# One free slot between two steps of the compressed attention, and cross-attention scores formed up to four units ahead

## The chip, the core and the metric

The kernel runs on one core of a Trainium2 chip. The core has TensorE (PE: matrix products, which are also used to turn tiles over), VectorE (DVE), ScalarE (ACT), GpSimd (POOL) and a queue (SP) that issues the loads. Each engine works through its own instructions in the order of the program and waits at semaphores for the others. The metric is device time in microseconds (us), median of the runs; lower is better.

## What is computed

Two layers of a first block, then two layers of a second block, on 512 rows of width 1024, all in float32:

```python
for i in range(DEPTH):                       # first block, DEPTH = 2
    ...                                      # projections, gated linear recurrence
    s_cmp = jnp.einsum('bgntd,bgcd->bgntc', q_nope, kc) * scale      # 31 compressed keys
    p_cmp = masked_softmax(s_cmp, cmp_mask)
    o_cmp = jnp.einsum('bgntc,bgcd->bgntd', p_cmp.astype(vc.dtype), vc)
    o_slc = selected_attn(q_rope, k_sl, heads(vsl, KVH), sel, scale)
    o_win = window_attn(q_rope, k_wn, heads(vwn, KVH), scale)
    o_nsa = gates[0] * o_cmp + gates[1] * o_slc + gates[2] * o_win
    ...
for l in range(DEPTH):                       # second block
    ...                                      # mixer
    s = jnp.einsum('bshd,bmhd->bhsm', q, k).astype(jnp.float32) * (XA_HEAD_DIM ** -0.5)
    p = jax.nn.softmax(s, axis=-1).astype(v.dtype)                   # 4 heads, 256 memory rows
    o = jnp.einsum('bhsm,bmhd->bshd', p, v).reshape(B, S, D_MODEL)   # and o @ wo
    ...                                      # feed-forward
```

## The kernel before

A product of float32 numbers is made of three products of parts: high times high, high times low, low times high. So every operand is split in two. A weight chunk of 128x1024 is loaded by SP into `raw`, its high part is cut by ACT (L2010) and its low part by POOL (L2682). A tile that TensorE has turned over (matrix product with `ident`, L762 and L1037 in block one, L1758 in block two) is read from its PSUM bank by ACT, which writes the high part, and then by DVE, which writes the low part (L1392, L2265). Only after DVE's read is the bank free ("evacuated").

The work of each layer is a list of steps, made by `steps_one` and `steps_two`. All five engines walk through the same list, and each does its part of every step (`step_...` functions of the same name for each engine). A step placed later in the list is thus later on every engine. A PSUM bank is given to each tile in advance: tiles with the same set of banks take turns, and a tile may be written only when the one before it in that bank has been evacuated (class `Groups`).

**Block one, attention.** `attention_steps` writes the list in slots. One slot holds in most cases: `turn` (a 128x128 piece of the shares of four heads is turned over), `exp` of the scores of the slot before, `recip`, one or two `score` (row j, PE L1023, L1024, L1026), `weigh` (DVE L1717 makes a factor, POOL L2674 multiplies the row by it), at most one step of the list `compressed`, and `value` (three products with the turned shares, L1050 to L1052) of the turn two slots earlier. The first turn of a unit waits for POOL's multiplication of the unit's last row (`pn_ready`). There are 40 turns, numbered `t`, for 4 tiles of 128 queries (`qt`).

For every `qt` there are four compressed steps, one in each of four slots in a row: `c_score` (PE L993, then DVE), `c_exp` (ACT L1318), `c_weigh` (six DVE instructions, L1688 to L1693) and `c_turn` (PE L1003: eight turns of the weighted shares into two banks, then ACT L1123 copies them). TensorE's `c_turn` waits for `cp_ready`, which the last of the six DVE instructions (L1693, 128x248 into `decays`) gives. The tiles of `c_turn`, of `c_score` and of `turn` take turns in the banks 7, 0, 1.

**Block two, cross-attention.** A unit is one head `hh` and one tile `qt` of 128 queries: 16 units, `u = 4 * hh + qt`. Four things are done for a unit: `scores(u)` (PE L1959, six products of 128x256), `greatest(u)` (DVE L2528) and `probs(u)` (ACT L2211, exponential into `Px`), `shares(u)` (DVE L2534 and L2535, division by the sum), `probs_turn(u)` (PE L1758, two turns, banks 3 and 4 in turn) with ACT L2062 and DVE L2265 (`PxT`) reading them out. Step `("xatt", hh, qt)` forms the scores of unit u + 2 and turns the shares of unit u + 1; DVE does shares(u + 1), greatest(u + 2) and the reading of unit u. Step 3 and below are mixed with chunks of other products (L1869, L1803), steps 6 and 7 are followed by one chunk of the queries of the last head each (`xq`, 24 products, L1803), and after each head comes `xout` (L1991, 12 products of 128x512, which need all four `PxT` of the head). Steps 8 to 15 have nothing between them but `xout`.

Of the kernel before, what the change touches and what calls it, by code (L numbers as in the profile page):

```python
# [210 lines left out]
def attention_steps():  # L211
# [10 lines left out]

    weighed, sent = set(), set()
    while t < len(TURNS):
        if not out:
            compressed = [("c_score", 0), ("c_exp", 0), ("c_weigh", 0), ("c_turn", 0)]
# [4 lines left out]
        if turned:  # L231
            slot += [("turn", t)]
            t += 1
            if qt and kt == 0 and (g, br) == (0, 0):
                compressed = [(kind, qt) for kind in ("c_score", "c_exp", "c_weigh", "c_turn")]
# [14 lines left out]
        slot += compressed[:1]  # L250
# [177 lines left out]

def groups_two(step):
# [28 lines left out]
    if kind == "xatt":  # L458
        hh, qt = step[1:]
        return [(("xs", hh, qt), (0, 1)), (("xp", hh, qt), (3, 4))]  # L460
# [5 lines left out]
def build(nc, d, out, counts):  # L466
# [3 lines left out]
    with ExitStack() as ctx:  # L470
# [169 lines left out]
        Px = sb("Px", [P, 2, MEM], where=xat)  # L640
# [1107 lines left out]
        def tensor_two(pe, l):  # L1748
# [214 lines left out]
            def probs_turn(u):  # L1963
                name = ("xp", *divmod(u, TT))
                pe.wait_ge(*px_ready.at(l, u + 1))
                turn(name, MT, lambda i: Px[:, u % 2, i * P:(i + 1) * P])

            def step_xatt(step):
                hh, qt = step[1:]
                u = hh * TT + qt  # L1970
                if u == 0:
                    pe.wait_ge(*G.evacuated(("xk", KD - 1), l))
                    scores(0)
                    scores(1)
                    probs_turn(0)
                if u + 2 < XH * TT:
                    scores(u + 2)
# [34 lines left out]
        def scalar_two(act, l):  # L2012
# [195 lines left out]
            def probs(u):  # L2208
                name = ("xs", *divmod(u, TT))
                act.wait_ge(*nm_ready[1].next(l))  # L2210
                nc.scalar.activation(Px[:, u % 2, :], G.ps(name)[:, 0:MEM], ACT.Exp, bias=nmx[:, u % 4:u % 4 + 1],  # L2211
# [7 lines left out]
            def step_xatt(step):  # L2219
                hh, qt = step[1:]  # L2220
                u = hh * TT + qt
                if u == 0:
                    probs(0)
                    probs(1)
                turned(u)
                if u + 2 < XH * TT:
                    probs(u + 2)
# [16 lines left out]
        def vector_two(dve, l):  # L2244
# [285 lines left out]
            def shares(u):  # L2530
# [4 lines left out]
                ts(Px[:, u % 2, :], Px[:, u % 2, :], recx[:, c], None, ALU.mult).then_inc(*px_ready.up())  # L2535

            def step_xatt(step):
                hh, qt = step[1:]
                u = hh * TT + qt
                if u == 0:  # L2540
                    greatest(0)
                    greatest(1)
                    shares(0)
                if u + 1 < XH * TT:
                    shares(u + 1)
                if u + 2 < XH * TT:
                    greatest(u + 2)
# [293 lines left out]
```

## Time and profile before

| | us |
|---|---|
| median of 3 runs (3026.43 to 3032.96) | 3026.7 |
| the profiled execution | 3025.9 |
| its span in the trace | 3024.0 |
| TensorE busy in the span | 2798.5 |
| VectorE busy | 1227.6 |
| ScalarE busy | 1284.9 |
| GpSimd busy | 1153.1 |

The profile is that of one execution. Its span is the time from the first to the last recorded instruction; 1.9 us of the run's time lie outside it. Times in the trace are counted from the start of the span. "Idle before" an instruction is the time in which its engine had nothing to do, and the name behind the arrow is what ended it. The mean granted clock of TensorE over the span was 0.964 of its full speed, which has two levels: 2.4 GHz (1.0) and 1.2 GHz (0.5).

### The profile page before, as it was taken

How to read it: one execution, taken by the hardware profiler on the slowest of the kernel's cores; microseconds unless marked ns; L12 is line 12 of the kernel's file. 1: busy time of each engine (PE TensorE's matmuls, PEld its weight loads, DVE VectorE, ACT ScalarE, POOL GpSimd, SP SyncE). 2: the span in 40 equal slices, each digit the busy share in tenths (PEclk: the TensorE clock that was granted, in tenths of full speed). 3: DMA queues.
4: the chain of work that ended last, by engine and by line, in shares of the span. 5: the costliest groups of instructions: out<-in, count | busy, mean ns of one | idle time of the engine just before them, and what ended most of it. 6: DMA issues, size and time to landing. Idle time of an engine off the chain costs nothing.

```text
span 3024.0 us, 40461 instructions
## 1 busy us (share of the span) xinstructions
PE 2798.5 (93%) x13636; PEld 2326.6 (77%) x13636; DVE 1227.6 (41%) x2186; ACT 1284.9 (42%) x2191; POOL 1153.1 (38%) x537
## 2 busy tenths in 40 slices
PE   8978789998778999899998999999899999899998
PEld 6777658777765788688786888888678887788887
DVE  4755771375567223434333331322442423232132
ACT  4443653554465353353443442334244444243243
POOL 3313334331234343244452344444234444244442
PEclk9989799999979999999999999999999999999999
DMA  5212102321210232133331233333223333133333
GB/s 148 63 44 63 42 1 84 96 70 37 64 56 1 63 109 83 42 98 105 105 112 49 84 105 98 98 98 109 63 75 93 91 116 101 56 93 103 91 98 98
DMA packets 269778, 242.32 MB, mean 80 GB/s; under 512 B 29376, under 2 KB 201600, under 8 KB 269568
## 3 DMA queue, kind: packets, MB, share of 16 engines
q1 hardware_dynamic: 266672, 235.12, 26.9%
q10 hardware_dynamic: 2896, 4.52, 0.5%
q8 instruction: 118, 1.93, 0.3%
q14 instruction: 92, 0.75, 0.1%
HBM read 237.51 MB, written 2.10 MB: 79 GB/s over the span
## 4 chain that ended last, share of the span: by engine, by line
issue 47%; PE 25%; POOL 25%; DVE 1%; ACT 1%; POOLq 0%; DMA 0%; DVEq 0%; ACTq 0%
POOL wlo L2682 23%; PE bank L1869 4%; PE bank L1873 4%; PE bank L1872 4%; PE bank L1807 3%; PE bank L1803 3%; PE bank L1806 3%; PE bank L1758 1%; POOL Ql L2674 0%; PE bank L1991 0%; POOL dE L2674 0%; POOL Kl L2674 0%; PE bank L1037 0%; POOLq L2681 0%; POOL vv L2674 0%
## 5 line engine op out<-in xcount | busy, mean ns | idle before, releaser
L2682 POOL TENSOR_TENSOR wlo<-raw,whi 128x1024 fp32r<-128x1024 f32 (+2 forms) x440 | 1057.4, 2408 | 1684.4 <-ACT whi L2010 1684.2
L2010 ACT CAST whi<-raw 128x1024 fp32r<-128x1024 f32 (+2 forms) x443 | 456.1, 1034 | 710.9 <-PE bank L1869 465.8
L1803 PE MATMUL bank<-xhi,whi 128*128 128x512 f32 x928 | 365.3, 394 | 0.3 <-issue 0.3
L1807 PE MATMUL bank<-xhi,wlo 128*128 128x512 f32 x928 | 363.1, 391 | 0.0
L1806 PE MATMUL bank<-xlo,whi 128*128 128x512 f32 x928 | 363.0, 391 | 0.0
L1869 PE MATMUL bank<-whi,xhi 128*128 128x512 f32 x832 | 329.2, 396 | 9.7 <-POOL wlo L2682 5.8
L1872 PE MATMUL bank<-wlo,xhi 128*128 128x512 f32 x832 | 326.4, 392 | 0.0
L1873 PE MATMUL bank<-whi,xlo 128*128 128x512 f32 x832 | 326.2, 392 | 0.0
L776 PE MATMUL bank<-whi,xhi 128*128 128x512 f32 (+2 forms) x704 | 263.3, 374 | 3.1 <-DVE pT L1392 3.1
L779 PE MATMUL bank<-wlo,xhi 128*128 128x512 f32 (+2 forms) x704 | 257.7, 366 | 0.0
L780 PE MATMUL bank<-whi,xlo 128*128 128x512 f32 (+2 forms) x704 | 257.2, 365 | 0.0
L1803 PEld LDWEIGHTS bank<-xhi,whi 128*128 128x128 f32 x928 | 175.4, 189 | 38.0 <-issue 1.7
L1807 PEld LDWEIGHTS bank<-xhi,wlo 128*128 128x128 f32 x928 | 175.2, 189 | 36.8
L1806 PEld LDWEIGHTS bank<-xlo,whi 128*128 128x128 f32 x928 | 175.4, 189 | 36.1
L1869 PEld LDWEIGHTS bank<-whi,xhi 128*128 128x128 f32 x832 | 157.7, 190 | 44.1 <-POOL wlo L2682 6.6
L1873 PEld LDWEIGHTS bank<-whi,xlo 128*128 128x128 f32 x832 | 157.6, 189 | 33.3
L1872 PEld LDWEIGHTS bank<-wlo,xhi 128*128 128x128 f32 x832 | 157.9, 190 | 32.1
L776 PEld LDWEIGHTS bank<-whi,xhi 128*128 128x128 f32 x704 | 136.2, 194 | 24.8 <-DVE pT L1392 3.6
L780 PEld LDWEIGHTS bank<-whi,xlo 128*128 128x128 f32 x704 | 135.1, 192 | 20.9
L779 PEld LDWEIGHTS bank<-wlo,xhi 128*128 128x128 f32 x704 | 135.7, 193 | 19.4
L2374 DVE TENSOR_TENSOR h<-h,bank 128x512 f32<-128x512 f32 x64 | 44.0, 688 | 249.6 <-PE bank L1873 249.6
L1869 PE MATMUL bank<-whi,gT 128*128 128x512 f32 x352 | 137.4, 390 | 1.6 <-DVE et L2367 1.6
(492 smaller groups left out, 4995.9 us busy)
## 6 DMA issues: line engine op xcount, KB each, us to landing
raw<-in_w_in SPq DMA_DIRECT2D x147, 512.0 KB, 3.7
raw<-in_w SPq DMA_DIRECT2D x132, 512.0 KB, 3.8
raw<-in_w_pg SPq DMA_DIRECT2D x16, 512.0 KB, 3.8
raw<-in_w_o SPq DMA_DIRECT2D x16, 512.0 KB, 3.8
raw<-in_xa_k SPq DMA_DIRECT2D x16, 512.0 KB, 3.9
raw<-in_xa_v SPq DMA_DIRECT2D x16, 512.0 KB, 3.8
raw<-in_xa_q SPq DMA_DIRECT2D x16, 512.0 KB, 4.0
raw<-in_xa_o SPq DMA_DIRECT2D x16, 512.0 KB, 3.8
```

The source lines that it names most:

```text
L776: mm = pe.matmul(o, a, wh, start=(i == 0 and kk_ == 0), stop=False)
L779: pe.matmul(o, a, wl, start=False, stop=False)
L780: mm = pe.matmul(o, b, wh, start=False, stop=(i == n - 1 and kk_ == nk - 1))
L1803: mm = pe.matmul(o, wh, rhs[0][:, k, :], start=(k == 0), stop=False)
L1806: pe.matmul(o, wh, rhs[1][:, k, :], start=False, stop=False)
L1807: mm = pe.matmul(o, wl, rhs[0][:, k, :], start=False, stop=(k == KD - 1))
L1869: mm = pe.matmul(G.ps(name)[:, :], a, wh, start=(i == 0 and kk_ == 0), stop=False)
L1872: pe.matmul(G.ps(name)[:, :], a, wl, start=False, stop=False)
L1873: mm = pe.matmul(G.ps(name)[:, :], b, wh, start=False, stop=(i == n - 1 and kk_ == nk - 1))
L2010: nc.scalar.copy(whi[:, j % SLOTS, 0:nk * cols], raw[:, j % SLOTS, 0:nk * cols]).then_inc(hi_split, 1)
L2374: tt_(at, at, G.ps(name)[:, :], ALU.add).then_inc(*G.empty(name))
L2682: nc.gpsimd.tensor_tensor(wlo[:, s, 0:n], raw[:, s, 0:n], whi[:, s, 0:n].bitcast(F32), ALU.subtract).then_inc(lo_split, 1)
```

## The change

In block one an empty slot (`None`) is put between `c_weigh` and `c_turn`. In block two the scores run ahead by up to four units instead of two, but only from step 4 on: `scored_to` gives the last unit whose scores are formed by step u. Steps 0 to 3 form the same units as before, step 4 forms 6 and 7, step 5 forms 8 and 9, steps 6 to 11 one each, steps 12 to 15 none. The score tiles of units 6 and above take turns in the banks 2, 7, 0, 1 instead of 0, 1, and `Px` has four places instead of two.

```diff
+    def compressed_steps(qt):
+
+        return [("c_score", qt), ("c_exp", qt), ("c_weigh", qt), None, ("c_turn", qt)]
...
-        slot += compressed[:1]
+        slot += compressed[:1] if compressed and compressed[0] else []
         compressed = compressed[1:]
...
+def scored_to(u):
+
+
+    return min(u + (2 if u < 4 else 3 if u == 4 else 4), XH * TT - 1)
+
+
+def scored_in(u):
+    return range(scored_to(u - 1) + 1 if u else 0, scored_to(u) + 1)
...
-        return [(("xs", hh, qt), (0, 1)), (("xp", hh, qt), (3, 4))]
+        return [(("xs", *divmod(u, TT)), (0, 1) if u < 6 else (2, 7, 0, 1)) for u in scored_in(hh * TT + qt)] + [(("xp", hh, qt), (3, 4))]
...
-        Px = sb("Px", [P, 2, MEM], where=xat)
+        Px = sb("Px", [P, 4, MEM], where=xat)
...
-                    scores(0)
-                    scores(1)
-                    probs_turn(0)
-                if u + 2 < XH * TT:
-                    scores(u + 2)
+                for v in scored_in(u):
+                    scores(v)
+                    if v == 1:
+                        probs_turn(0)
                 if u + 1 < XH * TT:
                     probs_turn(u + 1)
...
-                if u == 0:
-                    greatest(0)
-                    greatest(1)
-                    shares(0)
-                if u + 1 < XH * TT:
-                    shares(u + 1)
-                if u + 2 < XH * TT:
-                    greatest(u + 2)
+                for v in scored_in(u):
+                    if v > 1:
+                        shares(v - 1)
+                    greatest(v)
+                    if v == 1:
+                        shares(0)
+                if scored_to(u) == XH * TT - 1 and len(scored_in(u)):
+                    shares(XH * TT - 1)
                 at = (slice(None), slice(None), slice(qt * P, (qt + 1) * P))
```

ScalarE's `step_xatt` reads out the turned tile of unit u first and then takes the exponentials of the units of `scored_in(u)`.

Below, lines of the changed kernel have numbers 13 or 14 higher than the same lines before.

TensorE, block one, slot of turn 27 (`qt` 3), before, from the score's last product (`causal`): the turns of `c_turn` (source `decays`) stand right behind it, ahead of the value products (source `Pt`).

```order
L1026 MATMUL bank<-causal,identb 128x128
L1001 REGISTER_ALU [waits cp_ready]
L1003 MATMUL bank<-ident,decays 31x128 [waits emptied1]
L1003 MATMUL bank<-ident,decays 31x128 x3
L1001 REGISTER_ALU
L1003 MATMUL bank<-ident,decays 31x128 [waits emptied7]
L1003 MATMUL bank<-ident,decays 31x128 x3
L1050 MATMUL bank<-Pt,vhi 128x512 [waits emptied1]
L1051 MATMUL bank<-Pt,vlo 128x512
L1052 MATMUL bank<-Pt,vhi 128x512
L1034 REGISTER_ALU
L1035 REGISTER_ALU [waits pn_ready]
```

The same place now, from the first value product on:

```order
L1064 MATMUL bank<-Pt,vhi 128x512 [waits emptied1]
L1065 MATMUL bank<-Pt,vlo 128x512
L1066 MATMUL bank<-Pt,vhi 128x512
L1048 REGISTER_ALU
L1051 MATMUL bank<-ident,Ql 128x128 [waits emptied1,pn_ready]
L1051 MATMUL bank<-ident,Ql 128x128
L1051 MATMUL bank<-ident,Kl 128x128 x2
L1034 REGISTER_ALU
L1037 MATMUL bank<-khh,qhl 128x512 [waits emptied4]
L1038 MATMUL bank<-kll,qhl 128x512
L1040 MATMUL bank<-causal,identb 128x128
L1015 REGISTER_ALU [waits cp_ready]
```

Three value products, one turn (which waits for POOL, `pn_ready`) and one score have moved ahead of `c_turn` and its wait. The DVE work of `c_weigh` has not moved.

TensorE, block two, from the end of `xout` of head 0 through steps 4 and 5, before (`kx8,qx8` are scores, `ident,Px` the turns of the shares):

```order
L1991 MATMUL bank6<-PxT,vx 128x512 x6
L1954 REGISTER_ALU
L1959 MATMUL bank0<-kx8,qx8 128x256 x6
L1965 REGISTER_ALU
L1758 MATMUL bank4<-ident,Px 128x128 x2
L1954 REGISTER_ALU
L1959 MATMUL bank1<-kx8,qx8 128x256 x6
L1965 REGISTER_ALU
L1756 REGISTER_ALU
L1758 MATMUL bank3<-ident,Px 128x128 x2
```

and now:

```order
L2004 MATMUL bank6<-PxT,vx 128x512 x6
L1968 REGISTER_ALU
L1973 MATMUL bank2<-kx8,qx8 128x256 x6
L1968 REGISTER_ALU
L1973 MATMUL bank7<-kx8,qx8 128x256 x6
L1979 REGISTER_ALU
L1772 MATMUL bank4<-ident,Px 128x128 x2
L1968 REGISTER_ALU
L1970 REGISTER_ALU
L1973 MATMUL bank0<-kx8,qx8 128x256 x6
L1968 REGISTER_ALU
L1973 MATMUL bank1<-kx8,qx8 128x256 x6
```

The scores of units 6 and 7 stand ahead of the first turn, those of 8 and 9 ahead of the next one (bank 3, behind the last row shown); before, it was one unit's scores ahead of each turn.

VectorE, block two, from the first division of step 4, before (`nmx` is the greatest score, `recx` the reciprocal of the sum, `PxT` the reading of the turned tile):

```order
L2535 TENSOR_SCALAR Px<-Px,recx 128x256
L2528 TENSOR_REDUCE nmx<-bank0 128x1
L2262 REGISTER_ALU
L2265 TENSOR_TENSOR PxT<-bank3,PxT 128x2x128
L2532 REGISTER_ALU
L2534 RECIPROCAL recx<-sumx 128x1
L2252 REGISTER_ALU
L2535 TENSOR_SCALAR Px<-Px,recx 128x256
L2528 TENSOR_REDUCE nmx<-bank1 128x1
```

and now:

```order
L2548 TENSOR_SCALAR Px<-Px,recx 128x256
L2540 REGISTER_ALU
L2541 TENSOR_REDUCE nmx<-bank2 128x1
L2545 REGISTER_ALU
L2547 RECIPROCAL recx<-sumx 128x1
L2265 REGISTER_ALU
L2548 TENSOR_SCALAR Px<-Px,recx 128x256
L2540 REGISTER_ALU
L2541 TENSOR_REDUCE nmx<-bank7 128x1
L2275 REGISTER_ALU
L2278 TENSOR_TENSOR PxT<-bank3,PxT 128x2x128
```

The reading of a turned tile (`PxT`), which frees bank 3 or 4, now stands behind a second division and a second search for the greatest. It is so in steps 4 and 5; in step 11 it stands behind one more division.

## Rows read from the trace of the kernel before

**Rows 1.** The page: the span and TensorE's busy time.

```profile
span 3024.0 us, 40461 instructions
PE 2798.5 (93%) x13636; PEld 2326.6 (77%) x13636; DVE 1227.6 (41%) x2186; ACT 1284.9 (42%) x2191; POOL 1153.1 (38%) x537
```

**Rows 2.** Waits of PE, whole span: us in total, times, longest us.

```profile
PE bank L1758 <- DVE Px L2535: 25.8, 24, 2.3
PE bank L1003 <- DVE decays L1693: 19.4, 8, 3.1
```

**Rows 3.** Timeline, layer 0, `qt` 1, PE: start us, us, instruction [idle before].

```profile
371.51 1.53 PE L1003 MATMUL bank<-ident,decays 128*31 128x128 f32 x8 [3.08 <-DVE decays L1693]
...
376.32 0.60 PE L1037 MATMUL bank<-ident,vv 128*128 128x128 f32 x4
```

**Rows 4.** Timeline, the same place, DVE and POOL.

```profile
369.15 0.41 DVE L1688 SCALAR_TENSOR_TENSOR decays<-k_cbias,decays 128x248 f32<-128x248 f32 x1
...
371.29 0.68 DVE L1392 TENSOR_TENSOR Pt<-bank,Pt 128x512 fp32r<-128x512 f32 x1
...
369.31 1.14 POOL L2674 TENSOR_TENSOR vv<-vv,coef 128x512 f32<-128x512 f32 x1 [2.72 <-DVE coef L1717]
```

**Rows 5.** Timeline, layer 0, `qt` 3, PE and POOL.

```profile
425.94 1.14 POOL L2674 TENSOR_TENSOR Kl<-Kl,coef 128x512 f32<-128x512 f32 x1 [2.71 <-DVE coef L1717]
...
428.13 1.06 PE L1003 MATMUL bank<-ident,decays 128*31 128x128 f32 x8 [2.97 <-DVE decays L1693]
...
429.72 0.38 PE L1037 MATMUL bank<-ident,Ql 128*128 128x128 f32 x2
...
431.45 0.38 PE L1037 MATMUL bank<-ident,Ql 128*128 128x128 f32 x2
```

**Rows 6.** Timeline, layer 0, `qt` 2, PE.

```profile
396.91 1.06 PE L1003 MATMUL bank<-ident,decays 128*31 128x128 f32 x8 [2.76 <-DVE decays L1693]
...
402.94 0.43 PE L1037 MATMUL bank<-ident,dE 128*128 128x128 f32 x2 [0.56 <-POOL Ql L2674]
```

**Rows 7.** Timeline, layer 0, `qt` 0, PE.

```profile
348.23 1.91 PE L1003 MATMUL bank<-ident,decays 128*31 128x128 f32 x8 [0.87 <-DVE decays L1693]
...
354.32 0.65 PE L1037 MATMUL bank<-ident,Ql 128*128 128x128 f32 x4 [1.42 <-POOL Ql L2674]
```

**Rows 8.** Timeline, layer 0, cross-attention from step 4 on, PE.

```profile
1606.64 0.87 PE L1959 MATMUL bank<-kx,qx 128*128 128x256 f32 x6
1608.67 0.44 PE L1758 MATMUL bank<-ident,Px 128*128 128x128 f32 x2 [1.15 <-DVE Px L2535]
...
1620.46 0.43 PE L1758 MATMUL bank<-ident,Px 128*128 128x128 f32 x2 [1.99 <-DVE Px L2535]
...
1627.84 2.88 PE L1991 MATMUL bank<-PxT,vx 128*128 128x512 f32 x12
...
1637.88 3.02 PE L1991 MATMUL bank<-PxT,vx 128*128 128x512 f32 x12 [0.23 <-DVE PxT L2265]
...
1647.55 5.04 PE L1991 MATMUL bank<-PxT,vx 128*128 128x512 f32 x12 [1.00 <-DVE PxT L2265]
```

**Rows 9.** Timeline, the same stretch, DVE.

```profile
1608.86 0.41 DVE L2265 TENSOR_TENSOR PxT<-bank,PxT 128x256 fp32r<-128x256 f32 x1
1609.58 0.17 DVE L2534 RECIPROCAL recx<-sumx 128x1 f32<-128x1 f32 x1 [0.30 <-ACT Px L2211]
...
1611.09 0.17 DVE L2534 RECIPROCAL recx<-sumx 128x1 f32<-128x1 f32 x1 [0.30 <-ACT Px L2211]
```

**Rows 10.** Timeline, layer 1, cross-attention, PE.

```profile
2561.16 0.87 PE L1959 MATMUL bank<-kx,qx 128*128 128x256 f32 x6
...
2574.95 0.43 PE L1758 MATMUL bank<-ident,Px 128*128 128x128 f32 x2 [1.99 <-DVE Px L2535]
...
2580.73 2.88 PE L1991 MATMUL bank<-PxT,vx 128*128 128x512 f32 x12
...
2601.03 4.51 PE L1991 MATMUL bank<-PxT,vx 128*128 128x512 f32 x12 [1.00 <-DVE PxT L2265]
```

More of the change, by code:

```diff
@@ L225, in attention_steps @@
         if not out:
-            compressed = [("c_score", 0), ("c_exp", 0), ("c_weigh", 0), ("c_turn", 0)]
+            compressed = compressed_steps(0)
         slot = []
@@ L234, in attention_steps @@
             if qt and kt == 0 and (g, br) == (0, 0):
-                compressed = [(kind, qt) for kind in ("c_score", "c_exp", "c_weigh", "c_turn")]
+                compressed = compressed_steps(qt)
         slot += [("exp", i) for i in scored]
@@ L1965, in probs_turn @@
                 pe.wait_ge(*px_ready.at(l, u + 1))
-                turn(name, MT, lambda i: Px[:, u % 2, i * P:(i + 1) * P])
+                turn(name, MT, lambda i: Px[:, u % 4, i * P:(i + 1) * P])
             def step_xatt(step):
@@ L2210, in probs @@
                 act.wait_ge(*nm_ready[1].next(l))
-                nc.scalar.activation(Px[:, u % 2, :], G.ps(name)[:, 0:MEM], ACT.Exp, bias=nmx[:, u % 4:u % 4 + 1],
+                nc.scalar.activation(Px[:, u % 4, :], G.ps(name)[:, 0:MEM], ACT.Exp, bias=nmx[:, u % 4:u % 4 + 1],
                                      accum_out=sumx[:, u % 4:u % 4 + 1]).then_inc(*G.empty(name))
@@ L2221, in step_xatt @@
                 u = hh * TT + qt
-                if u == 0:
-                    probs(0)
-                    probs(1)
-                turned(u)
-                if u + 2 < XH * TT:
-                    probs(u + 2)
+                for v in scored_in(u):
+                    if v == u + 2 or (v > 1 and v == scored_in(u)[0]):
+                        turned(u)
+                    probs(v)
+                if not len(scored_in(u)):
+                    turned(u)
             def step_xout(step):
@@ L2534, in shares @@
                 link(nc.vector.reciprocal(recx[:, c], sumx[:, c]))
-                ts(Px[:, u % 2, :], Px[:, u % 2, :], recx[:, c], None, ALU.mult).then_inc(*px_ready.up())
+                ts(Px[:, u % 4, :], Px[:, u % 4, :], recx[:, c], None, ALU.mult).then_inc(*px_ready.up())
             def step_xatt(step):
@@ L2539, in step_xatt @@
                 u = hh * TT + qt
-                if u == 0:
-                    greatest(0)
-                    greatest(1)
-                    shares(0)
-                if u + 1 < XH * TT:
-                    shares(u + 1)
-                if u + 2 < XH * TT:
-                    greatest(u + 2)
+                for v in scored_in(u):
+                    if v > 1:
[5 more added lines that the diff above has]
+                    shares(XH * TT - 1)
                 at = (slice(None), slice(None), slice(qt * P, (qt + 1) * P))
```

## The prediction

> **What bounds the kernel now.** TensorE does: it is busy for 93% of the span, the next engine for 42% [rows 1]. So I read the list of its waits first: only what shortens a wait of TensorE, or lets it run at its higher clock, can move the time. The two largest entries that the change touches are the turns of the cross-attention shares (L1758 waiting for the division L2535, 25.8 us in 24 waits) and the turns of the compressed shares (L1003 waiting for L1693, 19.4 us in 8 waits) [rows 2]. The change removes no work, so 45.2 us is about all that is at stake, apart from the clock. Then the timeline around each wait, for every engine that feeds it: the question there is what is late next.
>
> **Block one: the eight waits of `c_turn`.** I take `qt` 1, 2, 3 and 0 in turn; layer 1 repeats layer 0 (8 waits, 19.4 us, against 9.7 us in the four rows of layer 0 [rows 3, 5, 6, 7]).
>
> `qt` 1. TensorE stands idle for 3.08 us up to 371.51 [rows 3], that is from 368.43, while DVE works through the six instructions of `c_weigh`, which began at 369.15 and made room for the next one at 371.29 [rows 4]. The edit leaves those where they are and puts a value product, a turn and a score ahead of TensorE's wait. Their price, from `qt` 3: turn, score and value together take 431.45 - 429.72 = 1.73 us, `c_turn` with its value product 429.72 - 428.13 = 1.59 us [rows 5]; half of the latter is the value (0.8), so turn and score are 0.9. The value product can run at once, to 369.2. The turn is the first of a unit and waits for POOL's row, which ends at 369.31 + 1.14 = 370.45 [rows 4]: a new, shorter wait of 1.2 us. Turn and score end at 371.4, when `cp_ready` is there, `c_turn` and a value end at 373.0, and the next turn, which needs its bank read by DVE (L1392, now directly behind `c_weigh` and once more behind ScalarE's copy), starts at about 373.3. Before, it started at 376.32 [rows 3]: 3.0 us saved. About half of that is clock: 371.51 to 376.32 is 4.8 us, while the same instructions took 3.3 us at `qt` 3 [rows 3, 5].
>
> `qt` 3. Idle from 425.16. Value to 425.96, POOL's row ready at 425.94 + 1.14 = 427.08, turn and score to 428.0, `c_turn` and value to 429.7, next turn 429.9 against 431.45 [rows 5]: 1.55 us saved. `qt` 2: value, turn and score (1.7 us) fit into the idle 2.76 us without a new wait for POOL, because this turn is not the first of a unit, and the factor that POOL waits for before 402.94 comes earlier too [rows 6]: 1.7 us. `qt` 0: there is 0.87 us in front of `c_turn` and 1.42 us in front of a turn that hangs on the same delayed scores [rows 7]; ScalarE's two copies now stand behind four exponentials, so I take 1.5 of the 2.3.
>
> Sum for a layer: 1.5 + 3.0 + 1.7 + 1.55 = 7.75 us, for two 15.5 us. Bounds: 19.4 + 2 x 1.5 (clock) = 22.4 if no new wait arose; 8 us if DVE and ScalarE, which have their own queues of turned tiles, hold back half of the shift. The other cost is nil: the copies are needed by `c_val`, which for `qt` 1 now comes one slot after `c_turn` instead of two, with some 1.3 us left.
>
> **Block two: steps 4 to 15.** Steps 0 to 3 are as before, so the waits in them stay. I count from the scores of step 4 (1606.64 in layer 0, 2561.16 in layer 1 [rows 8, 10]). One round of division, search for the greatest and exponential takes 1611.09 - 1609.58 = 1.5 us, and the reading of the turned tile (`PxT`) at 1608.86 to 1609.27 stands ahead of the second round [rows 9]. Now it stands behind it, and turns alternate between two banks, so the turn of step u + 1 waits for `PxT` of step u - 1:
> - Step 4: turn at +2.0 as before (same division, 1608.67 [rows 8]). Step 5: two scores of 0.7 to 0.9 us, to +3.7; the bank comes free at 2.6 + 1.5 = +4.2.
> - Step 6: `PxT` of step 5 is two rounds later, +7.3, while TensorE is ready at +5.2: a new wait of 2.1 us. The chunk behind it starts at +7.5.
> - Step 7: chunk 5.6, score 0.9, and no wait for the division, where 1.99 us stood before 1620.46. The next chunk starts at +14.1, as before, with two units' scores already made.
> - `xout` of head 1 at +19.8; before 1627.84 - 1606.64 = +21.2 in layer 0 and 2580.73 - 2561.16 = +19.6 in layer 1. The two layers differ by clock alone: the same 1.99 us of idle time was followed by 7.4 us up to `xout` in layer 0 and by 5.8 us in layer 1 [rows 8, 10].
> - Steps 8 to 11: each turn waits for a `PxT` round (0.6 to 1.0 us), and `PxT` of step 11 comes behind one more division, so `xout` of head 2 waits for it 2.5 us: 2.7 + 8.5 = 11.2 us from one `xout` to the next, before 1637.88 - 1627.84 = 10.0.
> - Steps 12 to 15 have only turns left: 6.4 us to the last `xout`, before 1647.55 - 1637.88 = 9.7.
>
> Together 19.8 + 11.2 + 6.4 = 37.4 us up to the last `xout`, before 40.9 and 39.9 [rows 8, 10]. The last `xout` itself was busy for 5.04 and 4.51 us where the others took 2.88 [rows 8, 10]: lower clock. With one stretch at the lower clock in each layer (1.6 us, from 7.4 against 5.8 above) it is 37.4 + 2.9 + 1.6 = 41.9, before 45.9 and 44.4: 4.0 and 2.5 us saved, 6.5 in all. Bounds: 45.9 + 44.4 - 2 x 40.3 = 9.7 us if no stretch falls; -3 us if each layer has two more of them and one more round than I count.
>
> On the clock the Trainium skill (TensorE: Matmul & The Clock Gate, Part 1: The HAM clock gate) says that the monitor looks at windows that run free of the kernel and do not begin anew with it. That fits the two layers above, with equal idle time and 1.6 us between them. By that rule no term of clock is safe, neither the 2 x 1.5 us of `qt` 1 nor the 1.6 us of each layer.
>
> **Sum.** 15.5 + 6.5 = 22.0 us. The profiled execution took 3025.9 us, so 3003.9; the median of the runs is 0.8 above it: 3004.7 us. `Px` has more room and the loads of weights are not moved: POOL had nothing to do before its chunk, and the chunks follow TensorE.
>
> **Rivals.**
> - Cross-attention gives nothing (chance 0.2): the new waits behind `PxT` are as long as the ones removed. The 2.1 and 2.5 us above speak for it, the bare last four steps (9.7 to 6.4) against. Time: 3026.7 - 15.5 = 3011.2.
> - The clock takes some back (0.15): the half-speed stretch of `qt` 1 stays in both layers (3.0), and one more falls in each cross-attention (3.2). Time: 3004.7 + 6.2 = 3010.9. For it: the new waits of 2.1 and 2.5 us are longer than the 1.99 us that went before the stretch in layer 0. Against: two of the waits of `c_turn`, of 2.76 and 2.97 us, were followed by `c_turn` at 1.06 us for eight, the full speed. This is what the rule of the page cited above would do here.
> - Block one moves its wait to DVE and ScalarE (0.12): half the gain, 8 us, with 6.5: 3012.2.
> - Both small (0.05): the wait stands one slot on, and cross-attention gives nothing; 3022.
> - Slower (0.04): one mechanism, the place of `PxT` behind a second division. If each of the seven turns of steps 5 to 11 stood one whole round (1.5 us) later than it did before and the last four gave nothing, it would cost 2 x 7 x 1.5 = 21 us, more than the 15.5: 3032. It decides from 1.1 us for a turn. Against it: the second round comes only in steps 4, 5 and 11; from step 6 on each step has one round, as before, and so has time to catch up.
>
> **How the numbers follow.** The forecast has 0.44. The range is to hold 8 in 10: down to 3026.7 - 22.4 - 5 = 2999, up to 3018, past the three first rivals; outside are both small, slower, and a part of the tails. A measurement of this kernel can tell about 0.2%, 6 us, from no change. Faster than 3020.7 are the forecast and the first three rivals less a tail: 0.88; within 0.2% 0.08; slower 0.04.
>
> **What would show it.** In the trace after: waits of L1017 (the new line of `c_turn`) of 1 us in all or less, new waits of about 1.2 us of the first turn of a unit for POOL at `qt` 1 and 3, and the attention of each layer 7 to 8 us shorter. In cross-attention: no wait for the division in steps 4 to 15 but that of step 4 (1.1 us), new waits of L1772 and of `xout` for `PxT` of about 2 us, and the last two `xout` 6 to 7 us apart. Wrong if the value product ahead of `c_turn` waits, if DVE reads its tiles no earlier after `qt` 1, or if `xout` of head 2 waits for more than 4 us.

## The result, and the profile after

| | before | after | ratio (95% interval) |
|---|---|---|---|
| median of 6 runs each, us | 3026.1 | 3005.6 | 0.9935 (0.992 to 0.9951) |
| runs, us | 3017.7 to 3033.0 | 3003.7 to 3008.9 | |
| span of the profiled execution, us | 3024.0 | 3001.9 | |

The forecast was 3004.7 us. The total came out within 1 us, but its terms did not all do so: in the traced execution block two gave 3.1 us of the 6.5 it was meant to give, and time in code that no edit touches made up for it.

The page of the kernel after, with the span and the busy time of the engines, beside [rows 1]:

```profile
span 3001.9 us, 40477 instructions
PE 2793.4 (93%) x13636; PEld 2321.5 (77%) x13636; DVE 1225.8 (41%) x2186; ACT 1283.4 (43%) x2191; POOL 1154.6 (38%) x537
```

The list of TensorE's waits after the change (us in total, times, longest us), beside [rows 2]. Lines have moved by 13 or 14: L1758 is L1772 now, L1003 is L1017, L1991 is L2004, L2265 is L2278, L2535 is L2548, L1693 is L1707:

```profile
PE bank L1772 <- DVE PxT L2278: 10.5, 12, 1.9
PE bank L1772 <- DVE Px L2548: 9.5, 6, 2.3
...
PE bank L2004 <- DVE PxT L2278: 6.7, 4, 2.3
...
PE bank L1017 <- DVE decays L1707: 2.3, 2, 1.1
```

The 19.4 us in front of `c_turn` are down to 2.3. The 25.8 us of waiting for the division are down to 9.5, but 17.2 us of waiting for `PxT` stand there now, where 2.6 us stood before: of 16.3 us taken from one wait, 14.6 came back in another.

**Where the 22.1 us of the two spans lie.** I compared the start of the same matmul, counted from the start of the program, in both traces; both have 13636 matmuls. A stretch's gain is how much closer its two ends stand. The second column is the changed kernel profiled once more.

| stretch (us in the trace before) | first trace after | second trace after | predicted |
|---|---|---|---|
| attention, layer 0 (339 to 450) | 7.5 | 7.3 | 7.75 |
| attention, layer 1 (882 to 996) | 7.3 | 8.0 | 7.75 |
| cross-attention from step 4, layer 0 (1606.6 to 1653.5) | 1.8 | 1.7 | 4.0 |
| cross-attention from step 4, layer 1 (2561.2 to 2607) | 1.3 | 1.3 | 2.5 |
| all the rest | 4.2 | -1.4 | 0 |
| the two spans | 22.1 | 16.9 | 22.0 |

The rest holds no instruction that the change moves. It is made mostly of pieces of 0.6 to 3.1 us of either sign, most of them where a stretch at the lower clock stands in one trace and not in the other, and it changed sign between two traces of one kernel.

**Block one after.** Timeline of layer 0, PE, at `qt` 1 (the first three rows), `qt` 2 and `qt` 3, and then POOL at `qt` 1 (columns as in [rows 3]):

```profile
368.41 0.66 PE L1051 MATMUL bank<-ident,vv 128*128 128x128 f32 x4 [1.33 <-POOL vv L2687]
...
369.40 1.15 PE L1017 MATMUL bank<-ident,decays 128*31 128x128 f32 x8
...
371.12 0.66 PE L1051 MATMUL bank<-ident,vv 128*128 128x128 f32 x4
...
391.75 1.15 PE L1017 MATMUL bank<-ident,decays 128*31 128x128 f32 x8 [1.15 <-DVE decays L1707]
...
420.08 0.44 PE L1051 MATMUL bank<-ident,Ql 128*128 128x128 f32 x2 [1.23 <-POOL Kl L2687]
...
421.11 1.11 PE L1017 MATMUL bank<-ident,decays 128*31 128x128 f32 x8
```

```profile
367.21 1.14 POOL L2687 TENSOR_TENSOR vv<-vv,coef 128x512 f32<-128x512 f32 x1 [2.72 <-DVE coef L1731]
```

`c_turn` waits for nothing at `qt` 1 and `qt` 3. The turn ahead of it waits 1.33 and 1.23 us for POOL: new waits, less than half as long as the 3.08 and 2.97 us in [rows 3, 5]. `c_turn` took 1.53 us in [rows 3] and takes 1.15 us here. The stretch at the lower clock behind the long wait, 371.9 to 375.3 us in the trace before, is gone: both traces without the slot (before, and block two alone below) have it in both layers, and none of the ten with one slot has it.

**Cross-attention after, from step 4's scores on.** PE, layer 0, then layer 1, beside [rows 8, 10]:

```profile
1587.07 1.59 PE L1973 MATMUL bank<-kx,qx 128*128 128x256 f32 x12
1589.09 0.44 PE L1772 MATMUL bank<-ident,Px 128*128 128x128 f32 x2 [0.43 <-DVE Px L2548]
...
1591.27 0.44 PE L1772 MATMUL bank<-ident,Px 128*128 128x128 f32 x2 [0.31 <-DVE PxT L2278]
...
1594.30 0.44 PE L1772 MATMUL bank<-ident,Px 128*128 128x128 f32 x2 [1.88 <-DVE PxT L2278]
...
1606.44 2.88 PE L2004 MATMUL bank<-PxT,vx 128*128 128x512 f32 x12
...
1617.65 5.49 PE L2004 MATMUL bank<-PxT,vx 128*128 128x512 f32 x12 [2.34 <-DVE PxT L2278]
...
1624.87 0.77 PE L1772 MATMUL bank<-ident,Px 128*128 128x128 f32 x4 [1.40 <-DVE PxT L2278]
1626.64 4.60 PE L2004 MATMUL bank<-PxT,vx 128*128 128x512 f32 x12 [1.00 <-DVE PxT L2278]
```

```profile
2540.42 1.59 PE L1973 MATMUL bank<-kx,qx 128*128 128x256 f32 x12
...
2561.41 2.88 PE L2004 MATMUL bank<-PxT,vx 128*128 128x512 f32 x12
...
2572.63 4.38 PE L2004 MATMUL bank<-PxT,vx 128*128 128x512 f32 x12 [2.34 <-DVE PxT L2278]
...
2580.50 3.01 PE L2004 MATMUL bank<-PxT,vx 128*128 128x512 f32 x12 [0.99 <-DVE PxT L2278]
```

The first two waits are short, then come 1.88 and 2.34 us for `PxT`. Right behind the second one the `xout` of head 2 takes 5.49 and 4.38 us; before the change it took 3.02 and 3.03. That is the lower of the two clocks: the view by stretches (stretch, us, busy time and count of PE, PEld, DVE, ACT and POOL, granted clock, DMA share, GB/s) gives a mean granted clock of 0.65 of full speed from 1617 to 1631, so the lower level held for some 70% of it.

```profile
1617.00:1631.00 14.00, 10.96 (x30) 8.20 (x31) 4.02 (x9) 3.02 (x7) 0.00 (x0) 0.65 0.00 1
```

### The profile page after: what moved, and what is told of

Read it like the earlier page. It is cut to its first block, busy times and chain, and to the rows that moved or that the text cites. A ratio compares the mean times of both kernels' runs of the same rounds, so it can differ in the third digit from the quotient of the medians.

```text
span 3001.9 us, 40477 instructions
## 1 busy us (share of the span) xinstructions
PE 2793.4 (93%) x13636; PEld 2321.5 (77%) x13636; DVE 1225.8 (41%) x2186; ACT 1283.4 (43%) x2191; POOL 1154.6 (38%) x537
## 4 chain that ended last, share of the span: by engine, by line
issue 47%; POOL 25%; PE 25%; DVE 1%; ACT 1%; POOLq 0%; DMA 0%; DVEq 0%; ACTq 0%
POOL wlo L2695 23%; PE bank L1883 4%; PE bank L1886 4%; PE bank L1887 4%; PE bank L1821 3%; PE bank L1820 3%; PE bank L1817 3%; PE bank L1772 1%; POOL Ql L2687 0%; PE bank L2004 0%; POOL vv L2687 0%; POOL dE L2687 0%; POOL Kl L2687 0%; POOL At L2687 0%; POOLq L2694 0%
```

## The experiments

### The two parts alone, and both again

Block one alone is the kernel before with

```
+    def compressed_steps(qt):
+
+        return [("c_score", qt), ("c_exp", qt), ("c_weigh", qt), None, ("c_turn", qt)]
...
-        slot += compressed[:1]
+        slot += compressed[:1] if compressed and compressed[0] else []
```

and block two alone is the changed kernel without the `None`.

> The kernel before with the empty slot alone; block two as before. Theory (parts add up, and what is left over is clock): each layer's attention is 7.2 to 7.5 us shorter, as in the trace after the change (14.7 us for two), so 3026 - 15 = 3011 us, ratio 0.995; what the difference to 3005.6 leaves, some 5 us, is block two with 3 and a clock that stands differently in stretches that no edit touches. The attention gives 14 to 15.5 us whatever the total does. Rival (the slot gives all of it, and cross-attention nothing): 3006 us, ratio 0.9935, and the 4 us of shift that the trace shows between the two attentions' end and cross-attention come back here. Rival (the clock gain of qt 1 is chance): one of the two layers gives 1.5 us less.

> The changed kernel without the empty slot: scores four units ahead alone. Theory: cross-attention from step 4 on gives 1 to 3 us a layer and no more, since waits for PxT take the place of waits for the division: 3026 - 3 = 3023 us, ratio 0.999; the last three xout stand 11.2 us and, at the higher clock, 6.4 us apart, with some 1.5 us more for each xout at the lower clock. As predicted: 6.5 us, 3019.5 us, ratio 0.9978. Rival (nothing): 3026 us and 1.0.

> The changed kernel again, on the chip and beside the runs of before that the parts alone have. Theory: ratio 0.9935 as before, the sum of the two parts alone within 3 us; the attention of block one gives 14.7 us again, cross-attention from step 4 on 1 to 4 us, and the shift outside both, 4.3 us in the first trace, comes out differently, between -4 and +5 us. Rival (the shift outside is a consequence of the change): it is 4 us again, with the stretches at the lower clock in the same places.

All beside the same runs of before (3025.9 us, 17 runs). The last two columns are how many us shorter a stage is than in the trace before:

| | median, us | ratio (95%) | attention, two layers | cross-attention from step 4, layers 0 and 1 |
|---|---|---|---|---|
| block one alone | 3012.5 (6 runs) | 0.9958 (0.9944 to 0.9973) | 14.7 in all | -0.2, -1.8 |
| block two alone | 3019.8 (12 runs) | 0.9981 (0.9971 to 0.999) | 0.0 and -3.5 | 2.6, 1.3 |
| both again | 3007.2 (6 runs) | 0.9935 (0.9921 to 0.9949) | 15.3 in all | 1.7, 1.3 |

13.4 and 6.1 us make 19.5, and both together give 18.7: the parts add up. Block one is worth 14.7 to 15.3 us in all three traces that have it, against the trace before. That the slot gives the whole falls: with it alone the ratio is 0.9958, and its interval leaves out 0.9935. But the trace before is one trace. The trace of block two alone runs the same attention without the slot, and its layer 1 took 3.5 us more: behind the waits of 2.75 and 2.97 us at `qt` 2 and 3 `c_turn` took 1.91 us, at the lower clock, where the trace before has 1.05 us behind waits of the same length. Against that trace the slot gives 18 us.

```profile
939.98 1.91 PE L1017 MATMUL bank<-ident,decays 128*31 128x128 f32 x8 [2.75 <-DVE decays L1707]
...
973.17 1.91 PE L1017 MATMUL bank<-ident,decays 128*31 128x128 f32 x8 [2.97 <-DVE decays L1707]
```

For block two the median (6.1 us) is near the forecast of 6.5, while the traces show 2.6 and 1.3 us in the two stages. The row of block one alone shows one reason why a trace is a poor yardstick here: its cross-attention runs the same instructions as the kernel before, and from step 4 on they took 0.2 and 1.8 us longer than in the profiled execution of before, with 10.2 us of granted half clock in each layer where that one had 10.2 and 6.8. Against this second trace the changed order gains 1.9 and 3.1 us, 5 in all. With the trace of the kernel with two empty slots below, four traces have the new order (from the scores of step 4 to the first matmul behind the last `xout`, 44.2 to 45.2 us in layer 0 and 44.5 to 44.7 in layer 1) and two the old (46.9 and 47.1, 45.8 and 47.6): the means differ by 4.4 us for the two layers. So block two gives 3 to 6 us, and one trace can't say more.

### Is it the place of `PxT` on DVE?

In the changed kernel DVE reads a step's turned tile behind all rounds of division and search for the greatest in that step; steps 4, 5 and 11 have two of the former. The next kernel puts the reading (`low()`) behind the first:

```
...
                 for v in scored_in(u):
                     if v > 1:
                         shares(v - 1)
                     greatest(v)
...
+                    if u > 3 and v == scored_in(u)[0]:
+                        low()
...
+                if u < 4 or not len(scored_in(u)):
+                    low()
```

> The changed kernel, with DVE's reading of the turned tile (PxT) in steps 4, 5 and 11 ahead of the second round of division and search for the greatest, no longer behind it. Theory (the turn of step u + 1 and xout wait for PxT behind the second round): the 1.88 us wait of the turn of step 6 falls to 0.3 to 0.7, the 2.34 us wait of xout of head 2 to about 1.2, together 2.5 to 3 us a layer, so 5 to 6 us less than the changed kernel, ratio to the kernel before 0.9918. Rival (the round itself is the bound: PE waits for DVE's rounds of 1.5 us wherever PxT stands): the waits move to the next turns and the total stays, 0 to 1 us a layer. Rival (the clock takes it): the waits go, and the xout of heads 2 and 3 stay at 4.4 to 5.5 us.

2999.0 us (5 runs), ratio 0.9908 (0.9893 to 0.9924), beside 3007.2 of both again on the same chip: 8.2 us less. PE's rows, layer 0 and then layer 1:

```profile
1600.06 0.44 PE L1772 MATMUL bank<-ident,Px 128*128 128x128 f32 x2 [0.90 <-DVE PxT L2278]
...
1612.26 2.88 PE L2004 MATMUL bank<-PxT,vx 128*128 128x512 f32 x12
...
1622.29 3.01 PE L2004 MATMUL bank<-PxT,vx 128*128 128x512 f32 x12 [1.15 <-DVE PxT L2278]
...
1628.80 4.60 PE L2004 MATMUL bank<-PxT,vx 128*128 128x512 f32 x12 [1.00 <-DVE PxT L2278]
...
2570.09 3.01 PE L2004 MATMUL bank<-PxT,vx 128*128 128x512 f32 x12 [1.15 <-DVE PxT L2278]
...
2576.60 3.03 PE L2004 MATMUL bank<-PxT,vx 128*128 128x512 f32 x12 [1.00 <-DVE PxT L2278]
```

The waits fell as expected, 1.88 to 0.90 and 2.34 to 1.15, and they did not move elsewhere: the place of `PxT` was the cause of that part of them. But the stages became 6.9 and 7.0 us shorter than before the change, 5.2 and 5.7 more than both again, where 2.5 to 3 were expected. The waits make 2.5 us a layer of it (0.31 + 0.98 + 1.19). The other 5.9 us of the 10.9 go with the clock: the `xout` of head 2 is back at 3.01 us, and the half clock from step 4 on fell from 17.0 us in both layers together to 3.4. These 13.6 us at half speed cost at most 6.8 us of time (an estimate: all of them spent on matmuls). With the full clock, the last two `xout` stand 6.5 us apart in both layers; the forecast had 6.4.

Then the two places apart: this kernel moves the reading in step 11 alone, and leaves the 1.88 us of step 6.

```
+                    if u == 11:
+                        low()
...
+                if u != 11:
+                    low()
```

> The changed kernel, with the reading of PxT ahead of the last division in step 11 alone; steps 4 and 5 stay as the change made them. It asks whether the wait of 2.34 us right in front of the xout of head 2 decides that xout's clock (4.35 to 5.49 us in six of six stages with that wait, 3.01 to 3.03 us in six of six with a wait of 0.23 to 1.15 us). Theory (it does): wait 1.15 us, the xout takes 3.0 us in both layers, head 3's follows 6.5 us later; with 1.2 us for the wait and 1.5 to 2.6 us for the clock that is 2.7 to 3.8 us a layer from step 4 on, 5.5 to 7.5 us in all against the changed kernel. Rival (the gaps of steps 4 to 7, of 1.88 us, bring the clock down later): the xout of head 2 stays at 4.4 us or more in at least one layer, and only 1.2 us a layer is gained.

3000.5 us (4 runs), ratio 0.9917 (0.99 to 0.9933), beside 3026.3 us of before (7 runs), as for the next three kernels. The `xout` of head 2 took 3.02 and 3.01 us behind a wait of 1.15 us. The gap of step 6 stands, so it is not that gap that lowers the clock there. Shortening the wait in front of that `xout` alone brought its clock back in both layers. The stages are 5.4 and 2.2 us shorter than before, 3.6 and 0.9 more than both again: in layer 1 the 1.2 us of the wait and the 1.4 us of this `xout` are partly eaten by a last `xout` of 4.60 us, where both again had 3.01.

### Earlier still

```
+                if u > 4:
+                    low()
                 for v in scored_in(u):
```

> The changed kernel, with the reading of PxT ahead of all rounds of its step from step 5 on (in step 4 behind the first). Theory (a turn waits for nothing but the PxT of the turn before last): the waits of 0.9 us in step 6 and of 0.88, 0.37 and 0.37 us behind the xout of head 1 go, but the xout of head 2 then stands behind the rounds of DVE, 1.5 us each, and comes 8.9 instead of 10.0 us after that of head 1; together 2 us a layer less than with the tile behind the first round: 3005.6 - 8 - 4 = 2994 us, ratio 0.989. Rival (the rounds bound these steps already): no more than tile behind the first round, 2999 us, ratio 0.991.

2998.8 us (4 runs), ratio 0.9917 (0.99 to 0.9933): no gain over the reading behind the first round (0.9908), as the rival said. My theory missed: the turns behind the `xout` of head 1 now wait 0.96 and 0.96 us, and the next `xout` comes 11.0 us after it, not 8.9. DVE, ScalarE and PE in this kernel:

```profile
1610.75 0.15 DVE L2547 RECIPROCAL recx<-sumx 128x1 f32<-128x1 f32 x1
...
1611.20 0.42 DVE L2541 TENSOR_REDUCE nmx<-bank 128x1 f32<-128x256 f32 x1
1612.51 0.42 DVE L2278 TENSOR_TENSOR PxT<-bank,PxT 128x256 fp32r<-128x256 f32 x1 [0.89 <-ACT PxT L2075]
1612.86 0.15 DVE L2547 RECIPROCAL recx<-sumx 128x1 f32<-128x1 f32 x1
```

```profile
1611.65 0.47 ACT L2224 ACTIVATE Px<-bank,nmx 128x256 f32<-128x256 f32 x1 [1.60 <-DVE nmx L2541]
...
1612.12 0.36 ACT L2075 CAST PxT<-bank 128x256 fp32r<-128x256 f32 x1
```

```profile
1617.29 4.49 PE L2004 MATMUL bank<-PxT,vx 128*128 128x512 f32 x12 [1.75 <-DVE PxT L2278]
```

The reading of `PxT` waits for ScalarE's copy of the same tile, and on ScalarE that copy is queued behind the next exponential, which waits for DVE's search. With the tile first, a round is search, exponential, copy, reading, division in a row: 1612.86 - 1610.75 = 2.11 us, where it was 1.5 us with the reading beside the exponential. The `xout` waited 1.75 us and took 4.49 and 4.37 us.

### One turn ahead of `xout`

The kernel with `PxT` behind the first round, and in the plan the first step of head 3 ahead of the `xout` of head 2:

```
+            if (hh, qt) != (3, 0):
+                s += [("xatt", hh, qt)] + (xv1[qt:qt + 1] if hh == 0 else [])
...
-        s += [("xout", hh)]
+        s += [("xatt", 3, 0)] * (hh == 2) + [("xout", hh)]
```

> The changed kernel with PxT read behind the first round, and the step of head 3's first tile ahead of the xout of head 2 on all engines. Theory (the 1.5 us wait of a turn behind that xout is DVE's, which reads the two banks of xout before it comes to PxT): that wait goes, the one of 1.0 us before the last xout stays, since a turn, a copy and PxT must follow one another there; 1.5 us a layer less than with PxT behind the first round alone: 2999 - 3 = 2996 us, ratio 0.9898. Rival (the turn now waits for its bank ahead of the xout and shifts the wait to there): the total stays, 2999 us, ratio 0.9908. The last xout at 3.0 us in both layers if a shorter wait keeps the higher clock.

2996.9 us (4 runs), ratio 0.9911 (0.9895 to 0.9928). The turn taken ahead waits 1.08 us for its bank, and the turn behind the `xout` still waits 1.51 us: this is now the next turn, whose `PxT` is again behind the reading of the two `xout` banks. From the `xout` of head 2 to that of head 3 it is 6.2 us, from 6.5. The rival holds for the waits: they moved by one turn, and from step 4 on they make 6.6 us a layer in either kernel. The 2 us of the medians are inside the intervals. In the traces the stage of layer 0 is 1.9 us shorter than with `PxT` behind the first round, and 1.6 us of that is its last `xout`, 3.01 us where it was 4.60.

### Two empty slots

```
-        return [("c_score", qt), ("c_exp", qt), ("c_weigh", qt), None, ("c_turn", qt)]
+        return [("c_score", qt), ("c_exp", qt), ("c_weigh", qt), None, None, ("c_turn", qt)]
```

> The changed kernel with two empty slots between weights and turn of the compressed shares. Theory (one slot left 1.15 us of waiting at qt 2 and none elsewhere; the margin of the copies is used up): qt 2 gains 1.1 us a layer, but at qt 1 c_turn and the first c_val now stand in one slot with only the value product between them, so c_val waits 1 to 2 us for ScalarE's and DVE's copies, and qt 0, 1 and 3 gain nothing: within 1 us a layer of the changed kernel, 3004 to 3007 us, ratio 0.9935. Rival (the wait for weights is the only one that counts): attention 1.1 us a layer shorter, 3003.3 us. Rival (c_val's wait and the later start of its gating cost more): 3 us a layer more, 3011 us, ratio 0.995.

3008.7 us (4 runs), ratio 0.9948 (0.9932 to 0.9965), an interval that overlaps that of one slot; in its trace the attentions give 6.4 and 6.3 us, where ten traces with one slot give 7.1 to 8.0. The last wait for the weights is gone, and this stands at `qt` 2 in its place:

```profile
395.76 0.44 PE L1037 MATMUL bank<-khh,qhl 128*128 128x384 f32 x1 [1.30 <-ACT Kl L1354]
```

A score waits 1.30 us for its bank, which ScalarE had not emptied. `c_val` did not wait at all, so that part of my theory was wrong. In layer 0 the rest of the loss is 1.7 us between `qt` 1 and `qt` 2 in instructions with no new wait: clock. A second slot gains nothing.

### The order of DVE's queue against the distance of the scores

One kind of wait of [rows 8, 10] was left in the changed kernel too: 1.99 us for the division, in step 3 (the one in step 7 is gone). DVE in the changed kernel, in front of the turn that waits 1.99 us at 1575.87:

```profile
1573.20 0.69 DVE L2362 SCALAR_TENSOR_TENSOR tA<-bank,tD 128x512 f32<-128x512 f32 x1 [7.66 <-PE bank L1821]
1574.58 0.69 DVE L2364 TENSOR_TENSOR qx<-tA,qx 128x512 fp32r<-128x512 f32 x1 [0.68 <-ACT qx L2130]
1575.19 0.15 DVE L2547 RECIPROCAL recx<-sumx 128x1 f32<-128x1 f32 x1
1575.38 0.35 DVE L2548 TENSOR_SCALAR Px<-Px,recx 128x256 f32<-128x256 f32 x1
```

ScalarE's exponential of this unit, and then the turn:

```profile
1565.62 0.19 ACT L2224 ACTIVATION_READ_ACCUMULATOR Px<-bank,nmx 128x1 f32 x1
```

```profile
1575.87 0.43 PE L1772 MATMUL bank<-ident,Px 128*128 128x128 f32 x2 [1.99 <-DVE Px L2548]
```

DVE was idle for 7.66 us while this division could have been made: its exponential was there at 1565.8. The division is written into the next step, and so stands in the queue behind a chunk's result that comes only at 1573.2. The next kernel divides in the step that made the scores:

```
                 for v in scored_in(u):
-                    if v > 1:
-                        shares(v - 1)
+                    if v == 2:
+                        shares(1)
                     greatest(v)
                     if v == 1:
                         shares(0)
+                    if v > 1:
+                        if v == scored_in(u)[0] or u == 0:
+                            low()
+                        shares(v)
...
```

The lines left out remove the separate last division and the old place of the reading. A second kernel has this order without the change's block two: the kernel before with the empty slot, scores two units ahead, and on DVE `greatest(u + 2)`, the reading of `PxT`, `shares(u + 2)`. A third has the new order and all steps of head 3 ahead of the last two `xout`.

> The changed kernel with another order on DVE in cross-attention: search for the greatest of unit v, reading of PxT, division of unit v, all in the step that made v's scores; no longer the division of v in the next step. In the trace after the change the wait of 1.99 us in step 3 stands because the division of unit 4, whose exponential was there at 1565.9, is queued behind the reading of a chunk's result at 1573.2 to 1575.2. Theory (queue order on DVE, not the distance of the scores, makes that wait): the 1.99 us go in both layers, with 0.4 us in step 4 and the gains of PxT read behind the first round; 2.5 to 3 us a layer less than with the tile behind the first round, 2999 - 5.5 = 2993.5 us, ratio 0.989; the stretch at the lower clock behind step 3, 1.6 us in four of six stages, goes as well where it stood. Rival (the wait moves to the next chunk, whose evacuation on DVE now stands behind a division that waits 0.9 us for ScalarE): within 1 us of 2999.

> The kernel before with the empty slot of block one and, in cross-attention, scores two units ahead as before, but each division on DVE in the step that made the scores. It asks what the four units are worth once DVE's order is right. Theory (the waits of 1.99 us in steps 3 and 7 and of 1.15 us in step 4 were DVE's order; only the waits between steps with nothing between them need the distance): these three go, 5.1 us a layer, 3012.5 - 10 = 3002 us, ratio 0.9922, less than the changed kernel without its scores four ahead. Rival (distance matters): steps 4 to 7 give back what step 3 gains, and it stays above 3007 us.

> The kernel with each division in its own step, and all four steps of head 3 ahead of the xout of head 2, so that the last two xout stand back to back. Theory: the waits of 1.51 and 1.00 us behind and ahead of the xout of heads 2 and 3 go, and three turns ahead wait for PxT at 0.5 to 0.8 us each: 0.5 to 1 us a layer less than division in its own step, and both xout at 3.0 us in both layers: about 2992 us, ratio 0.9887. Rival (a turn, ScalarE's copy and DVE's reading of PxT cost the same 1.5 us wherever they stand, as with one turn ahead): nothing, or with three waits of 1.5 us ahead 1.5 us a layer more and the xout at the lower clock: 2996 to 2999 us.

Beside 3023.7 us of before (7 runs), the stages in us shorter than in the trace before:

| | median, us (4 runs each) | ratio (95%) | steps 0 to 3, layers 0 and 1 | from step 4, layers 0 and 1 |
|---|---|---|---|---|
| two ahead, own division | 2994.2 | 0.9901 (0.9885 to 0.9918) | 3.8, 3.8 | 3.4, 3.3 |
| four ahead, own division | 2983.8 | 0.9864 (0.9848 to 0.9881) | 3.9, 2.2 | 9.4, 7.9 |
| and both `xout` last | 2984.2 | 0.9865 (0.9848 to 0.9881) | 3.8, 2.2 | 9.6, 8.1 |

Four ahead with the division in its own step: TensorE's waits, and the last two `xout`.

```profile
PE bank L1772 <- DVE PxT L2278: 7.3, 10, 1.5
...
PE bank L1772 <- DVE Px L2548: 4.7, 2, 2.3
...
PE bank L2004 <- DVE PxT L2278: 4.3, 4, 1.2
```

```profile
1613.84 3.03 PE L2004 MATMUL bank<-PxT,vx 128*128 128x512 f32 x12 [1.15 <-DVE PxT L2278]
...
1620.37 3.02 PE L2004 MATMUL bank<-PxT,vx 128*128 128x512 f32 x12 [1.00 <-DVE PxT L2278]
```

Of 26.7 us of waiting in cross-attention in the changed kernel (10.5 + 9.5 + 6.7) 16.3 are left, and the only waits for the division are those of 2.33 us in step 0. At 0.9864 this kernel beats my theory (0.989) and the rival: 40 us less than before, twice the gain of the change. All three times lie below what I expected (2993.5, 3002 and 2992 us). Between `PxT` behind the first round and the division in its own step the two traces differ by 9.5 us in cross-attention: 5.5 us are waits (21.8 to 16.3), and 3.4 us are clock (13.6 us of half clock to 6.8). The ratios, 0.9908 and 0.9864, differ by 13 us, with intervals of 5 us either way; where the last 4 us come from is open.

With two units ahead the waits of L1762, as the turn's line is in that kernel, fell from 26.5 us (block one alone) to 17.0, and the half clock in the two stages from 34.0 us to 20.4, another 6.8 us. The waits of 1.99 us in steps 3 and 7 are gone in it, so they were the order; the 1.15 us of step 4 are not, 1.35 us stand one step later, and these go only with the scores further ahead. So most of what was to be had in cross-attention was the order of DVE's queue: it gives some 17 us with two units ahead (ratio 0.9958 to 0.9901), and the distance of four gives 10.5 on top of it. Alone, on the old order, the distance gave 6.

With both `xout` last, three turns wait 0.37, 1.08 and 0.75 us ahead of them and no wait is left between them. Their 24 matmuls took 7.67 and 7.66 us, where twice 2.88 would be 5.8. The waits got shorter by about as much as the clock took:

```profile
1614.88 0.44 PE L1773 MATMUL bank<-ident,Px 128*128 128x128 f32 x2 [1.08 <-DVE PxT L2279]
1616.07 0.77 PE L1773 MATMUL bank<-ident,Px 128*128 128x128 f32 x4 [0.75 <-DVE PxT L2279]
1616.60 7.67 PE L2005 MATMUL bank<-PxT,vx 128*128 128x512 f32 x24
```

## Why the prediction was right, and where it was wrong

**Block one: right, step by step.** For a layer I had 1.5, 3.0, 1.7 and 1.55 us for `qt` 0 to 3. The traces have 1.15, 3.05, 1.9 and 1.4 in layer 0 and 0.9, 3.05, 1.9 and 1.4 in layer 1: 14.8 us against 15.5. The new waits for POOL were to be 1.2 us at `qt` 1 and are 1.33 and 1.23 us. The half of `qt` 1 that I put down to the clock came in both layers, and in the repeated trace. That the total of block one fits this well is in part the trace it was worked out from: in the other trace without the slot the clock fell at `qt` 2 and 3 of layer 1 too, and against that one the slot gives 3.5 us more. `c_turn` waits 2.3 us in all instead of 1: at `qt` 2 there was 2.76 us of idle time and 1.7 us of work to fill it, which leaves 1.06, and 1.15 stand there; I had the terms and listed the wrong remainder.

**Block two: the waits right, the clock behind them wrong.** From step 4's scores the turns of steps 4, 5 and 6 came at +2.0, +4.2 and +7.2 us (forecast 2.0, 4.2, 7.3; its 2.6 + 1.5 is 4.1), the `xout` of head 1 at +19.4 and +21.0 (19.8, with 1.6 for clock in a layer), the next 11.2 us later in both layers (11.2). The waits for `PxT` were 1.88 and 2.34 us (2.1 and 2.5); the wait of step 4's turn for the division was 0.43 us and not 1.1, since a second unit's scores now fill it.

The step that failed is the clock in "steps 12 to 15 have only turns left: 6.4 us": it was 9.0 and 7.9 us, because the `xout` behind the 2.34 us ran at the lower clock. The runs in which that wait was 1.15 us show 6.5. The term for it in the sum, one stretch of 1.6 us in each layer on top of 37.4 + 2.9 = 40.3, was too small: up to the end of the last `xout` the stages took 1626.64 + 4.60 - 1587.07 = 44.2 and 2580.50 + 3.01 - 2540.42 = 43.1 us, which is 3.9 and 2.8 above 40.3. The forecast counted on the clock to recover; the half clock from step 4 on was 10.2 and 6.8 us in the trace before and 10.2 and 6.8 again in the trace after.

I had named the mechanism, as the rival "the clock takes some back", with one more stretch in each cross-attention. I had argued against it from two waits of `c_turn` in block one, of 2.76 and 2.97 us, after which the clock stayed high. In cross-attention the clock was down behind the 2.34 us eight times out of eight, and the argument does not hold in block one either: in layer 1 of block two alone it fell behind the same two waits.

**The sum.** 14.8 + 3.1 is 17.9 us in the first trace, not 22.0. That execution's span is 22.1 us shorter only because the rest gave 4.2 us, and in the second trace the rest took 1.4: that the total came within 1 us is in part luck. By the medians of the two series of runs the change gives 20.4 and 18.7 us; both fit 17.9 and 22.0 within their intervals, so the time alone could not have told that block two was over-estimated.

**The other rivals.** That cross-attention gives nothing falls: 0.9981 (0.9971 to 0.999) with it alone. That block one moves its wait to DVE and ScalarE falls: 14.7 to 15.3 us came. The slower case, `PxT` behind a second division, had the right place: this is what cost the 2.34 us and the clock. But it came at two places in each layer and not at seven, so it took back a part and not the whole.

On the clock, the Trainium skill (TensorE: Matmul & The Clock Gate, Part 1: The HAM clock gate) says that the monitor's windows run free of the kernel. The traces agree where equal code came out differently: with `PxT` behind the first round, the last `xout` took 4.60 us in layer 0 and 3.03 us in layer 1 behind the same waits. I took from it that no term of clock is safe. That was too wide: in the 22 stages with a wait right in front of the `xout` of head 2, its clock followed the length of that wait. It was not wrong everywhere: `c_turn` behind its waits of 2.75 to 2.98 us ran at either clock.

## What to carry to other kernels

Before making work earlier on the engine that waits, look at the queue of the engine it waits for: the 1.99 us in front of the turn in step 3 were no lack of distance but a division queued behind a result that was not there yet, with 7.66 us of idle time ahead of it. When an operation is made twice in a step, ask what is queued behind the second. Price a new wait of 2 us in front of a block of matmuls with the clock that may follow, and judge a change of under 1% by landmarks in the traces as well as by the total, over more than one trace.

## What was not expected of the hardware

At one place the clock behind a wait was far more regular than I had taken it to be. The `xout` of head 2, twelve matmuls, in both layers of all twelve traces in which it stands by itself:

| wait right ahead of it | stages | it took |
|---|---|---|
| 2.34 us | 8 | 4.35 to 5.49 us |
| 1.75 us | 2 | 4.49, 4.37 us |
| 0.23 to 1.15 us | 12 | 3.01 to 3.03 us |
| none, but 1.08 us ahead of the one turn before it | 2 | 3.04, 3.01 us |

The sum of the waits from the `xout` of head 1 to that of head 2 sorts the stages the same way: 2.0 to 2.8 us where it ran at the full clock, 3.7 to 4.0 where it did not. In the kernel with both `xout` last, with no wait right ahead of them and a sum of 3.0 us, they ran at the lower clock. So which of the two decides is not settled by the table; that last kernel speaks for the sum. The last `xout` had a wait of 1.0 us right ahead in all 24 stages. Where the waits since the `xout` of head 2 add up to 3.4 to 3.7 us (two units ahead) it took 4.51 to 5.48 us, six times out of six; where they are 2.4 to 2.5 us it took 4.60 us in four stages and 3.01 to 3.03 in fourteen. So behind the longer waits the clock was down every time, and behind the shorter ones it went either way.

The lost clock can be as large as the wait itself: in the kernel with `PxT` behind the first round 5 us of waits took 5.9 us more with them.
